# A feed-forward stage of a streaming encoder layer: 18 of 22 gate and up pairs by Strassen's seven block products

## The chip, the core and the metric

The kernel runs on one core of one Trainium2 chip. The metric is device time in microseconds (us) of one execution; lower is better. PE is TensorE's matmul row in the profile, PEld its weight loads, DVE is VectorE, ACT is ScalarE, POOL is GpSimd, SP is SyncE, which issues most of the transfers.

## The reference, cut to what matters

One layer of a hybrid encoder: a half-weighted SwiGLU feed-forward, a conformer convolution beside a Mamba-2 scan, a second half-weighted feed-forward, a final norm. 640 tokens (512 of a prompt and 8 x 16 samples), width 1024, feed-forward width 2816, everything in fp32. What the change touches is the feed-forward alone:

```python
def swiglu_ffn(x, w_gate, w_up, w_down):
    return (jax.nn.silu(x @ w_gate) * (x @ w_up)) @ w_down

x = x + 0.5 * swiglu_ffn(rms_norm(x, norm_ffn1), ffn1_w_gate, ffn1_w_up, ffn1_w_down)
# ... convolution and scan branches, merged ...
x = x + 0.5 * swiglu_ffn(rms_norm(x, norm_ffn2), ffn2_w_gate, ffn2_w_up, ffn2_w_down)
```

## The kernel before

Activations lie transposed, features on the 128 partitions and the 640 tokens (T) along the free axis, in two halves of 320 (TH). A matmul is in a one-pass fp32 format; to keep accuracy each factor is split into a high and a low part, and a product is three matmuls: high x high, high x low, low x high. The high part of a weight block is a cast on ScalarE (`split_hi`, L402), the low part a subtraction on VectorE (`split_lo`, L746).

A **job** (L1192) makes one block of 128 output features for all tokens: 8 chunks of the inner dimension x 3 products x 2 token halves = 48 matmuls of 320 columns, into two PSUM banks of `psj`. Jobs alternate between two buffers b = 0, 1; two jobs with the same number are a **half** (the counter `half` of all semaphores counts pairs of jobs). A feed-forward stage `ffn(f)` has 22 **pairs** (b = 0 gate, b = 1 up) in parts of 8, 8 and 6; behind each part come the 8 down jobs that use its hidden blocks, with 8, 8 or 6 chunks each. The first pair (stage 1: `pair_of_jobs`, L1207, both jobs chunk by chunk) runs on x scaled with the norm's gain but without the norm's root: each gate and up block is multiplied with `rstd` when it leaves PSUM.

Each engine works its own queue in the order written; semaphores connect them. For a pair i VectorE has: the low part of the up weights, `gate_s` = PSUM x rstd (L791), the low part of the next gate weights, `up_s` (L795), `hid` = silu_g x up_s (L799), `h_lo` (L801). ScalarE has: high part, `silu_g` (L434), high part, `h_hi` (L437). A down job ends in `x` += 0.5 x PSUM on VectorE (L820). PE starts a job when its weights' low part is there (`lo_done`) and its buffer has been emptied (`evac_done[b]`):

```python
pe.wait_ge(lo_done, 2 * half + b + 3)
pe.wait_ge(evac_done[b], half + 1)
```

In the first pair the sum of squares is finished (L759), summed over partitions on PE (`token_sums`, L1227), and `rstd` made by VectorE (variance, L763), ScalarE (Ln and Exp, L416 and L418, each behind a load of its table) and three VectorE steps (L769, L771, L773). `gate_s` of the first pair is behind it in VectorE's queue. Weights come by SP in transfers of 512 KB (384 KB for the last down jobs) into `w_raw[b]`, each as soon as the low part of the last one in that buffer is made.

The middle stage between the two feed-forwards (L1285 to L1373 and more jobs of L1202) is not touched, but for the places of its tensors in memory.

## Time and profile before

| | before |
|---|---|
| median of 3 runs | 1932.58 us (1930.64 to 1932.74) |
| the profiled execution | 1932.49 us, its span 1930.7 us |
| PE busy | 1851.6 us (96%), 12359 matmuls |
| PE weight loads | 1807.6 us (94%) |
| DVE busy | 1131.2 us (59%) |
| ACT busy | 735.4 us (38%) |
| granted TensorE clock, mean | 0.972 of 2.4 GHz |
| HBM | 155 MB read, 16 MB written, 89 GB/s |

The span runs from the first to the last instruction of the profiled execution. In the profile's second part a digit is the busy share of a fortieth of the span (48 us) in tenths; stage 1 of the feed-forward is from 9 to 488 us, stage 2 from 1440 to 1918 us.

### The profile page before, as it was taken

To read this page: it belongs to the slowest core of one execution; us is meant where nothing else is said; L and a number is where in the kernel's file an instruction comes from. 1 tells how busy PE (TensorE), PEld (TensorE's weight loads), DVE (VectorE), ACT (ScalarE), POOL (GpSimd) and SP (SyncE) were. 2 spreads that over 40 slices of the span, in tenths; PEclk is the share of its full clock that TensorE was granted. 3 is DMA by queue.
4 is the path that set the end of the run, shared out by engine and by line. 5 is a ranking of instruction groups with operands and counts; after the bars stand their busy time and mean duration, and the time that the engine had idled before them with its cause. 6 is when DMAs were issued, how large, how long until landed. Compare 5 with 4: busy or idle time off the path is not lost.

```text
span 1930.7 us, 29246 instructions
## 1 busy us (share of the span) xinstructions
PE 1851.6 (96%) x12359; PEld 1807.6 (94%) x12359; DVE 1131.2 (59%) x1632; ACT 735.4 (38%) x1306; POOL 94.8 (5%) x149
## 2 busy tenths in 40 slices
PE   6999999999799999989999999998999999999996
PEld 6999999999788999989889998998999999999995
DVE  5342343334647888979898898764544333442344
ACT  5221221122467537635853763254233211221222
POOL 0000000000011011010101101000000000000000
PEclk9999999999899899899989989999999999999998
DMA  4222222223143244134425413231221222222212
GB/s 149 77 77 77 72 76 79 69 74 115 69 125 105 61 153 131 44 118 131 129 53 161 127 49 123 77 127 55 77 77 66 77 77 69 74 77 77 77 63 80
DMA packets 54611, 173.60 MB, mean 90 GB/s; under 512 B 7344, under 2 KB 7504, under 8 KB 54480
## 3 DMA queue, kind: packets, MB, share of 16 engines
q1 hardware_dynamic: 43920, 137.41, 21.0%
q0 software_dynamic: 10560, 34.31, 6.3%
q8 instruction: 98, 1.61, 0.3%
q14 instruction: 33, 0.27, 0.0%
HBM read 155.49 MB, written 16.20 MB: 89 GB/s over the span
## 4 chain that ended last, share of the span: by engine, by line
PE 90%; DVE 4%; ACT 4%; issue 2%; DMA 1%; ACTq 0%; DVEq 0%; SPq 0%; POOLq 0%
PE psj L1202 79%; PE psj L1218 2%; PE pd L1362 2%; PE pc L1343 1%; PE pab L1356 1%; DVE w_lo L746 1%; PE pd L1350 1%; PE pab L1227 1%; ACT w_hi L402 1%; PE pc L1373 1%; PE pd L1373 1%; DVE rstd L773 0%; DVE rstd L771 0%; DVE rstd L769 0%; PE pab L1328 0%
## 5 line engine op out<-in xcount | busy, mean ns | idle before, releaser
L1202 PE MATMUL psj<-xa_hi,w_hi 128*128 128x320 f32 x2592 | 612.1, 318 | 19.4 <-DVE w_lo L746 19.3
L1202 PE MATMUL psj<-xa_lo,w_hi 128*128 128x320 f32 x2592 | 596.6, 312 | 0.0
L1202 PE MATMUL psj<-xa_hi,w_lo 128*128 128x320 f32 x2592 | 595.7, 311 | 0.0
L1202 PEld LDWEIGHTS psj<-xa_hi,w_hi 128*128 128x128 f32 x2592 | 439.7, 190 | 35.2 <-DVE w_lo L746 21.8
L1202 PEld LDWEIGHTS psj<-xa_lo,w_hi 128*128 128x128 f32 x2592 | 439.3, 190 | 0.0
L1202 PEld LDWEIGHTS psj<-xa_hi,w_lo 128*128 128x128 f32 x2592 | 438.5, 190 | 0.0
L746 DVE TENSOR_TENSOR w_lo<-w_raw,w_hi 128x1024 fp32r<-128x1024 f32 (+2 forms) x256 | 292.0, 1140 | 145.0 <-ACT w_hi L402 138.0
L402 ACT CAST w_hi<-w_raw 128x1024 fp32r<-128x1024 f32 (+2 forms) x256 | 250.2, 977 | 283.3 <-PE psj L1202 278.7
L1202 PE MATMUL psj<-h_lo,w_hi 128*128 128x320 f32 x704 | 160.5, 309 | 0.0
L1202 PE MATMUL psj<-h_hi,w_lo 128*128 128x320 f32 x704 | 160.5, 309 | 0.0
L1202 PE MATMUL psj<-h_hi,w_hi 128*128 128x320 f32 x704 | 160.4, 309 | 0.0
L820 DVE SCALAR_TENSOR_TENSOR x<-psj,x 128x640 f32<-128x640 f32 x48 | 39.6, 825 | 170.1 <-PE psj L1202 170.1
L437 ACT CAST h_hi<-hid 128x640 fp32r<-128x640 f32 x44 | 32.1, 730 | 267.6 <-DVE hid L799 267.6
L1202 PEld LDWEIGHTS psj<-h_hi,w_lo 128*128 128x128 f32 x704 | 117.9, 188 | 0.0
L1202 PEld LDWEIGHTS psj<-h_hi,w_hi 128*128 128x128 f32 x704 | 117.9, 188 | 0.0
L1202 PEld LDWEIGHTS psj<-h_lo,w_hi 128*128 128x128 f32 x704 | 117.9, 188 | 0.0
L795 DVE TENSOR_TENSOR up_s<-psj,rstd 128x640 f32<-128x640 f32 x44 | 36.3, 825 | 137.3 <-PE psj L1202 137.3
L924 DVE SCALAR_TENSOR_TENSOR v<-ext_a,parc,v 128x512 f32<-128x512 f32 x240 | 114.7, 548 | 0.0
L924 DVE SCALAR_TENSOR_TENSOR v<-ext_a,parg,v 128x512 f32<-128x512 f32 x240 | 114.4, 548 | 0.0
L434 ACT ACTIVATE silu_g<-gate_s 128x640 f32<-128x640 f32 x44 | 32.6, 740 | 206.6 <-DVE gate_s L791 206.6
L791 DVE TENSOR_TENSOR gate_s<-psj,rstd 128x640 f32<-128x640 f32 x44 | 36.3, 826 | 113.4 <-PE psj L1202 113.3
L948 DVE SCALAR_TENSOR_TENSOR pair<-ext_b,parg,pair 128x512 f32<-128x512 f32 x72 | 53.9, 748 | 37.3 <-ACT ext_b L541 37.0
(218 smaller groups left out, 1968.9 us busy)
## 6 DMA issues: line engine op xcount, KB each, us to landing
w_raw<-in_w_gu SPq DMA_DIRECT2D x88, 512.0 KB, 3.2
w_raw<-in_w_mix SPq DMA_DIRECT2D x56, 512.0 KB, 3.2
w_raw<-in_w_down SPq DMA_DIRECT2D x32, 512.0 KB, 3.2
w_raw<-in_w_tail SPq DMA_DIRECT2D x32, 512.0 KB, 3.2
acb<-cum_dram POOLq DMA_DIRECT2D x20, 512.0 KB, 6.9
w_raw<-in_w_ssm SPq DMA_DIRECT2D x32, 256.0 KB, 2.7
w_raw<-in_w_down_last SPq DMA_DIRECT2D x16, 384.0 KB, 3.0
ach<-cum_dram POOLq DMA_DIRECT2D x40, 128.0 KB, 5.4
```

The lines of the kernel that those rows point to most:

```text
L402: nc.scalar.copy(w_hi[:, b, 0:width], w_raw[:, b, 0:width]).then_inc(hi_done, 1)
L434: nc.scalar.activation(silu_g[:], gate_s[:], ACT.Silu).then_inc(silu_ready, 1)
L746: nc.vector.tensor_tensor(w_lo[:, b, 0:width], w_raw[:, b, 0:width], w_hi[:, b, 0:width].bitcast(F32), ALU.subtract).then_inc(lo_done, 1)
L791: nc.vector.tensor_tensor(halved(gate_s[:]), job_out(0), halved(rstd[:]), ALU.mult).then_inc(evac_done[0], 1)
L795: nc.vector.tensor_tensor(halved(up_s[:]), job_out(1), halved(rstd[:]), ALU.mult).then_inc(evac_done[1], 1)
L820: nc.vector.scalar_tensor_tensor(xc, job_out(b), 0.5, xc, ALU.mult, ALU.add).then_inc(evac_done[b], 1)
L924: nc.vector.scalar_tensor_tensor(dst, src, w[:, w0 + j:w0 + j + 1], dst, ALU.mult, ALU.add).then_inc(conva_ready[c] if s and j == KA - 2 e ...
L948: nc.vector.scalar_tensor_tensor(conv_b[:, s, 0:TP], ext_b[:, s, j:j + TP], param(w0 + j), conv_b[:, s, 0:TP], ALU.mult, ALU.add).then_inc ...
L1202: last = nc.tensor.matmul(psj[:, b, u, 0:TH], w[:, b, cols], act_in[:, k, u * TH:(u + 1) * TH], start=(k == 0 and n == 0), stop=(k == chun ...
L1218: last = nc.tensor.matmul(psj[:, b, u, 0:TH], w[:, b, cols], act_in[:, k, u * TH:(u + 1) * TH], start=(k == 0 and n == 0), stop=(k == chun ...
L1362: last = nc.tensor.matmul(out, old_h[b][:, c * P:(c + 1) * P], bc[:, 1, TP + b * TS:TP + (b + 1) * TS], start=True, stop=True)
L1373: nc.tensor.matmul((pc, pd)[b % 2][:], b_one[b], xtl[:], start=True, stop=True).then_inc(hs_mm, 1)
```

## The change

In each stage the first ORD = 4 pairs stay as they are. The other 18 (runs of 4, 8 and 6, NSP = 18 a stage) are made by Strassen's algorithm in Winograd's form: the weights of a pair are a 2 x 2 matrix of blocks (gate, up; first and second half of the inner dimension), the normed input one of 2 x 2 (halves of the inner dimension; halves of the tokens). Seven products of 4 chunks x 3 matmuls take the place of eight. The products A11, S3, S1 and S2 each begin a bank; A22, A12 and S4 add onto banks that ScalarE has copied out or VectorE has combined in the meantime.

For that the kernel needs: the sums of weight blocks (`sum_sp`, 2048 elements a partition) and the split of 3584 elements a pair in five groups (`split_sp` and `low_sp`, 2048 elements before); combinations of the results on VectorE (`sp_v`, `sp_22`, `sp_21`, `sp_12`), a copy on ScalarE, and the silu in two halves; once a stage the normed input (`normed`, now with rstd), its block sums (`block_sum`) and the split of its seven blocks (`t_high`, `t_low`, 1280 elements each). The weights of a pair come in one transfer of 1 MB (`load_run`), alternately into `w_raw` and a new buffer. The pairs alternate between PSUM banks 0 to 3 (those of `psj`) and 4 to 7. The first pair of each stage leaves PSUM by two copies on ScalarE, and rstd is multiplied in later; half 1's gate weights have a buffer of their own. The load of the dt weights is issued by POOL behind the last product of stage 1. The diff, cut:

```diff
+ORD = 4
+KH = KM // 2
+RUNS = (PARTS[0] - ORD, *PARTS[1:])
+NSP = sum(RUNS)
+FFN_HALVES = ORD + len(PARTS) * (KM // 2)
...
+(Q_A11, Q_S3, Q_S1, Q_S2, Q_A22, Q_A12, Q_S4) = range(7)
+BANK = {Q_A11: 0, Q_S3: 1, Q_S1: 3, Q_S2: 2, Q_A22: 1, Q_A12: 0, Q_S4: 3}
+(X_11, X_T3, X_T1, X_T2, X_T4, X_21, X_22) = range(7)
+X_OF = {Q_A11: X_11, Q_S3: X_T3, Q_S1: X_T1, Q_S2: X_T2, Q_A22: X_T4, Q_A12: X_21, Q_S4: X_22}
+(W_A11, W_S31, W_S2, W_A, W_S4) = range(5)
+W_OF = {Q_A11: W_A11, Q_S3: W_S31, Q_S1: W_S31, Q_S2: W_S2, Q_A22: W_A, Q_A12: W_A, Q_S4: W_S4}
...
+            def load_run(f, r, first):
+                for j in range(RUNS[r]):
+                    n = NSP * f + sum(RUNS[0:r]) + j
+                    before = sp_before(n, sp_buffer)
+                    if before is not None:
+                        sp.wait_ge(sp_lo, 5 * before + 4)
+                    if j == 1:
+                        sp.wait_ge(lo_done, 2 * first + 2)
+                    if f == 1 and n == NSP:
+                        sp.wait_ge(job_done, 2 * FFN2_HALF + 4)
+                    sp.dma_start(sp_raw(n)[:] if sp_buffer(n) else sp_raw(n),
+                                 d["w_sp"][n]).then_inc(sp_raw_in[sp_buffer(n)], 16)
...
+            def split_sp(n, w):
...
+                if w in (W_A11, W_A):
+                    b = sp_buffer(n)
+                    act.wait_ge(sp_raw_in[b], 16 * len([m for m in range(n + 1) if sp_buffer(m) == b]))
+                else:
+                    act.wait_ge(sp_sum, 3 * n + {W_S31: 1, W_S2: 2, W_S4: 3}[w])
+                if n:
+                    act.wait_ge(sp_done, 7 * (n - 1) + {W_A11: 1, W_S31: 3, W_S2: 4, W_A: 6, W_S4: 7}[w])
...
+                nc.scalar.copy(group_of(w_hi_4, w3_hi, w), fp32_of(n, w)).then_inc(sp_hi, 1)
...
+                act.wait_ge(job_done, 2 * half + 3)
+                act.wait_ge(acc_ready, (Q_FFN1, Q_FFN2)[f] + KM)
+                nc.scalar.copy(halved(gate_s), job_out(0)).then_inc(evac_done[0], 1)
+                act.wait_ge(job_done, 2 * half + 4)
+                nc.scalar.copy(halved(up_s), job_out(1)).then_inc(evac_done[1], 1)
+                split_hi(half + 1, 1)
+                inverse_root((N_FFN1, N_FFN2)[f], 7 * f)
+                silu(0)
+                split_hi(half + 2, 0)
+                silu(1)
+                split_hi(half + 2, 1)
+                t_high(X_11, 4)
+                silu(2)
+                split_hi(half + 3, 0)
+                t_high(X_T3, 9)
+                t_high(X_T1, 10)
+                split_hi(half + 3, 1)
+                t_high(X_T2, 11)
+                t_high(X_T4, 12)
+                t_high(X_21, 8)
+                t_high(X_22, 8)
+                n0 = NSP * f
+                split_sp(n0, W_A11)
+                for i in range(ORD - 1):
+                    h_high(i, hid_buf[:, i], i)
+                silu(3)
+                split_sp(n0, W_S31)
+                split_sp(n0, W_S2)
+                split_sp(n0, W_A)
+                split_sp(n0, W_S4)
+                h_high(3, hid, 3)
...
+                    for j in range(length):
+                        n = n0 + j
+                        more = j + 1 < length
+                        if j:
+                            split_sp(n, W_S4)
+                            act.wait_ge(sp_c12, n)
+                            nc.scalar.activation(silu_g[:, TH:T], c12, ACT.Silu).then_inc(sp_silu, 1)
+                        if more:
+                            split_sp(n + 1, W_A11)
+                        if j:
+                            h_high(i0 + j - 1, hid, chunk0 + j - 1)
+                        act.wait_ge(sp_done, 7 * n + 2)
+                        if n:
+                            act.wait_ge(sp_d, n)
+                        if not j:
+                            act.wait_ge(hid_ready, q0 + i0)
+                        nc.scalar.copy(halved(mix_c), ps[:, sp_set(n):sp_set(n) + 2, 0:TH]).then_inc(sp_copied, 1)
+                        if more:
+                            split_sp(n + 1, W_S31)
+                            split_sp(n + 1, W_S2)
+                            split_sp(n + 1, W_A)
+                        else:
+                            split_hi(half, 0, PARTS[r] * P)
+                            split_hi(half, 1, PARTS[r] * P)
+                        act.wait_ge(sp_done, 7 * n + 6)
+                        act.wait_ge(hid_ready, q0 + i0 + j)
+                        nc.scalar.activation(silu_g[:, 0:TH], ps[:, sp_set(n), 0:TH], ACT.Silu).then_inc(sp_silu, 1)
...
+            def sum_sp(n, w):
+                raw, b = sp_raw(n), sp_buffer(n)
+                if n % NSP == 0:
+                    dve.wait_ge(hlo_ready, NFF * (n // NSP) + ORD - 1)
+                if n:
+                    dve.wait_ge(sp_lo, 5 * (n - 1) + w + 1)
+                    dve.wait_ge(sp_sum, 3 * (n - 1) + {W_S31: 2, W_S2: 3, W_S4: 3}[w])
+                if w == W_S31:
+                    dve.wait_ge(sp_raw_in[b], 16 * len([m for m in range(n + 1) if sp_buffer(m) == b]))
+                    nc.vector.tensor_tensor(w_sum[:, 0:2], raw[:, 1:3], raw[:, 0].unsqueeze(1).broadcast_to([P, 2, KH * P]),
+                                            ALU.add).then_inc(sp_sum, 1)
+                elif w == W_S2:
+                    dve.wait_ge(sp_sum, 3 * n + 1)
+                    nc.vector.tensor_tensor(w_sum[:, 2], w_sum[:, 1], raw[:, 1], ALU.add).then_inc(sp_sum, 1)
+                else:
+                    dve.wait_ge(sp_sum, 3 * n + 2)
+                    nc.vector.tensor_tensor(w_sum[:, 3], w_sum[:, 2], raw[:, 3], ALU.add).then_inc(sp_sum, 1)
+            def low_sp(n, w):
+                dve.wait_ge(sp_hi, 5 * n + w + 1)
+                nc.vector.tensor_tensor(group_of(four_lo, w3_lo, w), fp32_of(n, w),
+                                        group_of(four_hi, w3_hi, w).bitcast(F32), ALU.subtract).then_inc(sp_lo, 1)
...
+            def sp_v(n):
+                dve.wait_ge(sp_copied, n + 1)
+                dve.wait_ge(sp_done, 7 * n + 4)
+                if n:
+                    dve.wait_ge(sp_c12, n)
+                nc.vector.tensor_tensor(halved(mix_d), halved(mix_c), ps[:, sp_set(n) + 2:sp_set(n) + 4, 0:TH],
+                                        ALU.subtract).then_inc(sp_d, 1)
+            def sp_22(n, before):
+                dve.wait_ge(sp_d, n + 1)
+                dve.wait_ge(hhi_ready, before)
+                dve.wait_ge(hlo_ready, before)
+                nc.vector.tensor_tensor(hid[:, TH:T], mix_d[:, TH:T], mix_d[:, 0:TH], ALU.subtract).then_inc(sp_c22, 1)
+            def sp_21(n):
+                dve.wait_ge(sp_done, 7 * n + 5)
+                nc.vector.tensor_tensor(hid[:, 0:TH], bank(n, 1), mix_d[:, 0:TH], ALU.subtract).then_inc(sp_c21, 1)
+            def sp_12(n):
+                dve.wait_ge(sp_done, 7 * n + 7)
+                dve.wait_ge(sp_silu, 2 * n)
+                nc.vector.tensor_tensor(c12, bank(n, 3), mix_d[:, 0:TH], ALU.add).then_inc(sp_c12, 1)
+            def sp_hid(n):
+                dve.wait_ge(sp_c22, n + 1)
+                dve.wait_ge(sp_c21, n + 1)
+                dve.wait_ge(sp_silu, 2 * n + 2)
+                nc.vector.tensor_tensor(hid, silu_g, hid, ALU.mult).then_inc(hid_ready, 1)
...
+                def normed(c):
+                    cols = slice(c % KH * TH, (c % KH + 1) * TH)
+                    out = t_sum[:, X_11:X_T4 + 1:X_T4 - X_11, cols] if c < KH else t_sum[:, X_21:X_22 + 1, cols]
+                    nc.vector.scalar_tensor_tensor(out, halved(x[:, c]), gains[:, 2 * f:2 * f + 1, c],
+                                                   halved(rstd[:]), ALU.mult, ALU.mult).then_inc(t_step, 1)
...
+                variance((N_FFN1, N_FFN2)[f], DM, RMS_EPS)
+                split_lo(half + 1, 1)
+                newton(7 * f)
+                dve.wait_ge(evac_done[0], half + 2)
+                nc.vector.tensor_tensor(gate_s, gate_s, rstd[:], ALU.mult).then_inc(scaled, 1)
+                dve.wait_ge(evac_done[1], half + 2)
+                nc.vector.tensor_tensor(up_s, up_s, rstd[:], ALU.mult).then_inc(scaled, 1)
...
+                hidden(0)
+                gate(1)
+                split_lo(half + 2, 0)
+                normed(0)
+                normed(1)
+                up(1)
+                hidden(1)
+                split_lo(half + 2, 1)
+                for c in range(2, KM):
+                    normed(c)
+                gate(2)
+                split_lo(half + 3, 0)
+                block_sum(X_T3, X_T4, X_22, ALU.subtract, 8)
+                block_sum(X_T1, X_11, X_T4, ALU.subtract, 8)
+                up(2)
+                hidden(2)
+                split_lo(half + 3, 1)
+                block_sum(X_T2, X_22, X_T1, ALU.add, 10)
+                block_sum(X_T4, X_21, X_T2, ALU.subtract, 11)
+                t_low(X_11)
+                n0 = NSP * f
+                low_sp(n0, W_A11)
+                t_low(X_T3)
+                t_low(X_T1)
+                for i in range(ORD - 1):
+                    h_low(i, hid_buf[:, i], i)
+                gate(3)
+                sum_sp(n0, W_S31)
+                sum_sp(n0, W_S2)
+                low_sp(n0, W_S31)
+                t_low(X_T2)
+                low_sp(n0, W_S2)
+                up(3)
+                hidden(3)
+                t_low(X_T4)
+                sum_sp(n0, W_S4)
+                low_sp(n0, W_A)
+                h_low(3, hid, 3)
+                t_low(X_21)
+                low_sp(n0, W_S4)
+                t_low(X_22)
...
+                    for j in range(length):
+                        n = n0 + j
+                        more = j + 1 < length
+                        if j:
+                            sp_12(n - 1)
+                        if more:
+                            sum_sp(n + 1, W_S31)
+                        if j:
+                            sp_hid(n - 1)
+                            low_sp(n, W_S4)
+                        if more:
+                            low_sp(n + 1, W_A11)
+                            sum_sp(n + 1, W_S2)
+                        if j:
+                            h_low(i0 + j - 1, hid, chunk0 + j - 1)
+                        if more:
+                            sum_sp(n + 1, W_S4)
+                            low_sp(n + 1, W_S31)
+                        sp_v(n)
+                        sp_22(n, q0 + i0 + j)
+                        if more:
+                            low_sp(n + 1, W_S2)
+                        else:
+                            split_lo(half, 0, PARTS[r] * P)
+                        sp_21(n)
+                        if more:
+                            low_sp(n + 1, W_A)
+                        else:
+                            split_lo(half, 1, PARTS[r] * P)
...
+                def product(n, q):
+                    pe.wait_ge(sp_lo, 5 * n + W_OF[q] + 1)
+                    if n % NSP == 0:
+                        pe.wait_ge(t_lo_ready, 7 * f + X_OF[q] + 1)
+                    first = q in (Q_A11, Q_S3, Q_S1, Q_S2)
+                    if first:
+                        before = sp_before(n, sp_set)
+                        if before is not None:
+                            pe.wait_ge(sp_c12, before + 1)
+                            pe.wait_ge(sp_silu, 2 * before + 2)
+                    else:
+                        pe.wait_ge(sp_copied if q != Q_S4 else sp_d, n + 1)
+                    hi, lo = block_of(four_hi, w3_hi, q), block_of(four_lo, w3_lo, q)
+                    for k in range(KH):
+                        for m, (w, t) in enumerate(((hi, t_hi), (hi, t_lo), (lo, t_hi))):
+                            last = nc.tensor.matmul(ps[:, sp_set(n) + BANK[q], 0:TH], w[:, k * P:(k + 1) * P],
+                                                    t[:, X_OF[q], k * TH:(k + 1) * TH],
+                                                    start=(first and k == 0 and m == 0),
+                                                    stop=(k == KH - 1 and m == 2), skip_group_check=not first)
+                    last.then_inc(sp_done, 1)
...
+                    for j in range(RUNS[p]):
+                        if j < 2:
+                            pe.wait_ge(evac_done[0], half + 1)
+                            pe.wait_ge(evac_done[1], half + 1)
+                        for q in range(7):
+                            product(n0 + j, q)
```

## Rows read from the trace of the kernel before

**Rows 1.** The page: busy us and share; then 40 slices of PE and its clock.

```profile
PE 1851.6 (96%) x12359; PEld 1807.6 (94%) x12359; DVE 1131.2 (59%) x1632; ACT 735.4 (38%) x1306; POOL 94.8 (5%) x149
...
PE   6999999999799999989999999998999999999996
PEclk9999999999899899899989989999999999999998
```

**Rows 2.** The chain that ended last: start us, us, what; stage 2.

```profile
1457.86 452.38 PE psj L1202 x3072
```

**Rows 3.** Timeline of PE, stage 2: start us, us, instructions.

```profile
1453.42 0.46 PE L1202 MATMUL psj<-xa_hi,w_lo 128*128 128x320 f32 x2
1457.86 0.57 PE L1202 MATMUL psj<-xa_hi,w_hi 128*128 128x320 f32 x2 [3.98 <-DVE w_lo L746]
...
1462.73 0.46 PE L1202 MATMUL psj<-xa_hi,w_lo 128*128 128x320 f32 x2
...
1469.47 0.46 PE L1202 MATMUL psj<-xa_lo,w_hi 128*128 128x320 f32 x2
```

**Rows 4.** Windows: us, PE, PEld, DVE, ACT, POOL busy, PEclk, DMA share, GB/s.

```profile
45.00:143.00 98.00, 98.00 (x670) 98.00 (x670) 39.86 (x42) 23.49 (x28) 0.00 (x0) 1.00 0.22 75
...
590.00:605.00 15.00, 15.00 (x121) 13.92 (x119) 13.41 (x23) 12.66 (x36) 3.88 (x6) 1.00 0.60 175
```

**Rows 5.** Chain and groups of instructions, line 1343, middle stage.

```profile
604.18 1.02 PE pc L1343 x16
...
L1343 PE MATMUL pc<-mdec,xdt 128*64 128x128 f32 x320 | 22.8, 286 | 7.0 <-issue 7.0
```

**Rows 6.** Groups by form: busy us, mean ns of one, idle before; the two splits.

```profile
L746 DVE TENSOR_TENSOR w_lo<-w_raw,w_hi 128x1024 fp32r<-128x1024 f32 x208 | 254.7, 1225 | 141.5 <-ACT w_hi L402 134.5
...
L746 DVE TENSOR_TENSOR w_lo<-w_raw,w_hi 128x512 fp32r<-128x512 f32 x32 | 22.0, 687 | 0.0
...
L402 ACT CAST w_hi<-w_raw 128x1024 fp32r<-128x1024 f32 x208 | 217.3, 1045 | 201.8 <-PE psj L1202 197.4 <-DVE yb L1098 4.3
...
L402 ACT CAST w_hi<-w_raw 128x512 fp32r<-128x512 f32 x32 | 19.7, 616 | 81.5 <-PE psj L1202 81.2 <-DMA w_raw<-in_w_ssm 0.2
```

**Rows 7.** Timeline of DVE and of ACT in the first pair of stage 1.

```profile
15.22 0.88 DVE L778 SCALAR_TENSOR_TENSOR xa_lo<-x,gains,xa_hi 128x640 fp32r<-128x640 f32 x1
16.02 0.82 DVE L759 TENSOR_TENSOR acc<-acc,sq 128x640 f32<-128x640 f32 x1
...
18.28 0.88 DVE L778 SCALAR_TENSOR_TENSOR xa_lo<-x,gains,xa_hi 128x640 fp32r<-128x640 f32 x1
...
16.07 0.81 ACT L421 ACTIVATE xa_hi<-x,gains 128x640 fp32r<-128x640 f32 x1
```

**Rows 8.** Groups by form on ACT: two copies out of PSUM.

```profile
L656 ACT COPY z<-psj 128x640 f32<-128x640 f32 x16 | 11.0, 687 | 4.0 <-PE psj L1202 4.0
...
L536 ACT COPY ext_b<-psj 128x320 f32<-128x320 f32 x24 | 10.0, 415 | 0.0
```

**Rows 9.** Timeline of PE and of DVE at a job's end.

```profile
135.90 0.46 PE L1202 MATMUL psj<-h_hi,w_hi 128*128 128x320 f32 x2
...
136.10 0.82 DVE L795 TENSOR_TENSOR up_s<-psj,rstd 128x640 f32<-128x640 f32 x1 [3.24 <-PE psj L1202]
```

**Rows 10.** Timeline of PE, stage 1: end of the first pair, next job.

```profile
26.88 0.46 PE L1218 MATMUL psj<-xa_hi,w_lo 128*128 128x320 f32 x2
35.72 0.91 PE L1202 MATMUL psj<-xa_hi,w_hi 128*128 128x320 f32 x2 [8.38 <-DVE w_lo L746]
...
39.09 0.47 PE L1202 MATMUL psj<-xa_hi,w_hi 128*128 128x320 f32 x2
```

**Rows 11.** Timeline of ACT and DVE: stage 2's norm, from the exponential's table on.

```profile
1449.37 1.28 ACT L418 ACT_TABLE_LOAD   x1
1450.67 0.74 ACT L418 ACTIVATE pair<-pair 128x640 f32<-128x640 f32 x1
...
1452.30 0.82 DVE L771 TENSOR_TENSOR rstd<-rstd,pair 128x640 f32<-128x640 f32 x1
```

441 lines of the change are left out of this document (283 added, 158 removed).

## The prediction

> **What bounds the kernel now.** I read the page first. TensorE's matmul row is busy 96% of the span while VectorE has 59% and ScalarE 38%, and nearly every slice outside the two ends and the middle stands at 9 with the granted clock at 9 tenths or more [rows 1]. A busy PE row alone doesn't prove that PE sets the time, so the chain of waits comes next: each feed-forward stage is in it one unbroken piece of 3072 matmuls, 452.38 us long for stage 2 and 0.02 less for stage 1 [rows 2]. Inside it a pair of 128x320 matmuls starts every 0.293 us: 23 such pairs between 1462.73 and 1469.47 give 6.74/46 = 0.1465 us (0.1466 with the decimals of more rows) for one matmul at the full 2.4 GHz [rows 3], and 3072 x 0.1466 = 450.4 is all of the piece but 2.0. So in these stages nothing but the number of matmuls sets the time, no wait is left but one at each stage's start, and a window of the first stage has PE busy 98.00 of 98 us, VectorE 39.86, ScalarE 23.49 [rows 4]. These are what the change can spend.
>
> **Matmuls removed.** A pair now is two jobs of 8 chunks x 3 products x 2 token halves = 96 matmuls, 14.07 us. A changed pair has 7 products of 4 chunks x 3 = 84, 12.31 us. 36 pairs lose 12 each: 432 x 0.1466 = **-63.3 us**. What the two shapes differ in beside that is where a matmul writes: before, neighbours alternate between two banks, now 12 in a row add into the same one. No row shows that. The nearest is the 16 matmuls of line 1343, which go to one bank in 1.02 us, 0.064 each, though each record lasts 0.286 [rows 5]; a bank does not hold the next matmul until the last is written. They write other columns of it and do not add, so the ends are 0 and, if each waited for the end of a record of that length, 3024 x 0.14 = +420 us. I take 0: the nearest row shows no hold at all. The products' extra semaphore waits cost nothing where they are met: the jobs on the hidden blocks wait at each of their chunks of 6 matmuls and lie inside the same unbroken piece [rows 2].
>
> **What a run of changed pairs asks of VectorE.** From the two forms of the split, 1024 elements take 1.225 us and 512 take 0.687 [rows 6]: 0.15 + 1.05 ns an element, which fits the 0.82 shown for 640 [rows 7]; so 320 is taken as 0.49 and 1280 as 1.50. Where nothing is awaited, the next operation starts 0.09 before the recorded end of the last (0.88 at 15.22, the next at 16.02 [rows 7]). A pair needs 3 of 1024 (sum S3/S1, two splits), 5 of 512, 3 of 640 (difference, product, low part of the hidden block) and 3 of 320: 3.68 + 3.44 + 2.48 + 1.47 = 11.1 us by durations, 14 x 0.09 less = 9.8 by pitch, in 12.31 us of PE. ScalarE: 2 x 1.045 + 3 x 0.616 for the splits, 0.69 for the copy, 0.72 for the hidden block (the casts give 0.838 ns an element), 2 x about 0.42 for the half silus, as a copy of 320 [rows 6, 8] = 6.2 us. Both fit. The order matters as much: call t = 0 the start of a pair n on PE. ScalarE's last split for pair n+1 waits for the product A12 (10.56), ends 11.6, and VectorE, which stands in its queue at the low part of it, gets on at 11.65 and ends at 12.8, i.e. 0.5 into the next pair. From there to the end of the difference that product S4 needs lie 1 of 320, 2 of 1024, 3 of 640 and 4 of 512 by pitch, 7.3, with a wait of some 0.5 for the high part of S3/S1 at 6.35: done at 8.4, and PE wants it at 10.56. **2.1 us of slack**; by full durations 1.8 us is left. So I cost the runs at 0, with VectorE as the engine that would be late next. The weights come in one transfer of 1 MB a pair, issued about 12 us ahead: 85 GB/s beside 75 now at a DMA share of 0.22 [rows 4]. The transfer of the dt weights that POOL now issues behind the last product of stage 1 has the last 8 down jobs, 8 x 36 x 0.1466 = 42 us, as cover. The split put early into stage 1's prologue delays ScalarE's next inputs by 1.0 us, where it is 2.2 us ahead of VectorE (input 6: 16.07 against 18.28 [rows 7]): nothing.
>
> **After a down stage.** The first changed pair of a run writes the banks of the last down job, so it waits for the update of x. Now jobs alternate and nothing waits. From PE's last matmul to VectorE's start are 0.20 us (135.90 to 136.10), the update lasts as long as this operation, 0.82 [rows 9], and about 0.1 passes to PE: 1.13, four times: **+4.5 us**.
>
> **The start of each stage, taken away.** Now PE stands after the first pair, because its banks are emptied only with rstd: from 27.17 (26.88 + 2 matmuls) to 35.72, 8.55 us, and from 1453.71 to 1457.86, 4.15 us [rows 3, 10]. After each gap PE runs some matmuls at 1.2 GHz (0.267 a matmul): 12 in 3.37 us where 1.76 are due, and 22 in 4.87 where 3.23 are due, so 1.6 more each [rows 3, 10]. In the new kernel ScalarE copies the banks out without rstd. In stage 2 the first bank is free during the second job: the gap goes. In stage 1 both jobs end together: 0.2 + 0.69 + 0.06 = 0.95 stays, and I expect no half clock after it. **-(7.6 + 4.15 + 3.2) = -15.0 us**.
>
> **The start of each stage, added.** Before the first changed pair VectorE must scale the input, form the block sums of x and split all 7 of them, in the time of 3 ordinary pairs. Let T be the end of the first pair; then PE has work to T + 42.2 in stage 2, T + 43.2 in stage 1. rstd is later than now: ScalarE first copies (0.2 to 0.9) and splits (1.9), then loads a table (1.28), Ln (0.74), a table, Exp: 6.0 [rows 11]; three VectorE steps of 0.82 that read one another, 0.86 with the gap: **T + 8.6** (9.25 in stage 1). From there to up(3), the emptying of the last bank that the first product waits for, VectorE's queue holds 14 operations of 640 (2 scalings, 3 gates, 3 ups, 3 hidden, 3 low parts) x 0.74 = 10.4; 8 input scalings of 0.80 = 6.4; 6 of 1024 x 1.14 = 6.8; 8 of 1280 (4 block sums, 4 low parts) x 1.41 = 11.3; 3 of 512 x 0.60 = 1.8: 36.7. It stands for ScalarE four times: 1.9 for the high part of (3,0), 0.9 for that of (3,1), 3.15 at the first A11 split, which stands behind four casts of 1.26 on ScalarE, and 0.5 for S3/S1; and 0.12 more in each of some 6 steps that read the one before. 36.7 + 6.45 + 0.7 = 43.8, so up(3) ends at **T + 52.4**, though its job is done at 42.2. up(3) stands behind sums, splits and low parts that the first product does not need, and behind the wait of VectorE all of PE is queued. PE's stall: 10.15 in stage 2, 53.05 - 43.2 = 9.85 in stage 1. After it the clock has fallen as after the 8.38 gap [rows 10]: 1.6 each. Then VectorE has 13.5 us to the difference of pair 0 (the four things left over, 7 splits and sums of pair 1), T + 65.9, where PE wants to begin S4 at 52.4 + 10.56 + 1.6 = 64.6: 1.3 each. Together **20.0 + 3.2 + 2.6 = +25.8 us**. Bounds: by recorded durations instead of pitches 38 x 0.09 = 3.4 more in each stage and some 2 more at S4 (+11 in all); if the waits for ScalarE are half as long and the clock holds, 3 + 1.6 less each (-9).
>
> As to the pitch, the Trainium skill (VectorE: DVE Perf Modes, "The DRAIN you can't avoid") says that a next operation starts only once the pipe has emptied, whether or not a semaphore stands between. The trace has the next start 0.09 ahead of the recorded end even with a met wait between [rows 7]; by a reading of that rule that puts operations end to end the time would be the +11 above.
>
> **Sum** against the profiled execution (1932.49, its span 1930.7; the median of the runs is 1932.58, the same): -63.3 - 15.0 + 4.5 + 25.8 = -48.0, **1884 us**. Stage 1 comes out some 26 us shorter, stage 2 some 22, the rest as it is.
>
> **The rivals.**
> A, the forecast: PE-bound runs, one stall of about 10 us at each stage's start. 0.63.
> B, the starts cost little (VectorE faster through its queue, PE held only a few us): without the 25.8 it would be 1859; with a third of it 1867. For it: VectorE was idle over half of this stretch before. Against it: the queue is in order and up(3) is its 39th entry. 0.10.
> C, VectorE end to end at recorded durations: 1884 + 11 = 1895, and up to 1905 if single pairs lose a few tenths. For it: nearly every new operation carries a wait. Against it: the start at 16.02 [rows 7]. 0.15.
> D, slower: VectorE is late in each pair, and PE's gap before S4 drops the clock. Needed is that the way from the low part of A to the difference, 7.8 by pitch with its wait, grows beyond 9.9 (a quarter more). If then each of the 36 pairs pays 1.6 at 1.2 GHz and a few tenths of waiting, say 1.9, it is 1884 + 68 = 1952; it decides from 48.0/36 = 1.33 us a pair. For it: after 8.4 and after 4.0 us of waiting the clock did fall [rows 3, 10]. Against it: in the middle stage PE changes between groups of 24 and fewer matmuls with a wait at each, VectorE 89% busy, and the granted clock is 1.00 [rows 4]. 0.07. The Trainium skill (TensorE: Matmul & The Clock Gate, "A second HAM failure mode: psum-queue depth-cycling") tells of a kernel whose short idle times between matmul groups made the clock swing; by it the 252 products with their waits would bring this case. That window does not agree with it for groups of this size.
> E, adding into one bank 12 times in a row slows the matmul: 16 ns each (11%) on 3024 eats all 48.0 us. Also slower then, 1935 or above. 0.05.
> That the change does not do what it says I leave out: the loops give 84 matmuls.
>
> **How the numbers follow.** The likeliest is A, 1884. A's own bounds are 1875 to 1895; C adds 1905, B 1859. 1867 to 1902 leaves out D, E, half of B and the end of C, about 0.2. About 0.2% (4 us) is what a measurement can tell from no change. Faster: A, B, C and a share of E: 0.90. Same: 0.02. Slower: D and most of E, 0.08.
>
> **What would show it.** PE has 11927 matmuls. Within the runs a product takes 12 x 0.1466 = 1.76 us and 7 of them 12.3 with no gap. PE stands about 1 us after stage 1's first pair and not at all in stage 2. One gap of about 10 us before the first product of each stage, released by VectorE's up_s, 1.2 GHz for some 12 matmuls behind it. A gap of about 1.1 us at the start of the other four runs, released by the update of x. VectorE about 80 to 90% busy in the runs. Wrong would be: gaps before S4 in each pair, a pitch above 0.147 in the products, a clock under 1.00 in the runs, or a start gap far from 10.

## The result and the profile after

The changed kernel takes **1884.68 us** (median of 4 runs, 1880.54 to 1889.88) beside 1931.61 (1929.54 to 1932.74) for the kernel before on the same chip: ratio 0.976, 95% interval 0.9733 to 0.9786. The profiled execution took 1883.59 us, its span is 1881.8. The prediction was 1884.

The page: busy us, share, instructions; then the slices of PE, DVE and the clock, as in [rows 1].

```profile
PE 1789.4 (95%) x11927; PEld 1742.4 (93%) x11927; DVE 1331.1 (71%) x1958; ACT 853.0 (45%) x1504; POOL 94.8 (5%) x149
...
PE   7799999998899999999999999998999799999996
...
DVE  6863873774648888989899899765556854863754
...
PEclk9899999999889899899999989999999899999998
```

432 matmuls fewer, as counted. The cost shows in PE's slices: a 7 in the second slice and in the thirty-second where before there were 9s, each with an 8 in the clock row. VectorE is up from 59% to 71%.

The chain of waits (start us, us, what) has the stages in pieces now, where [rows 2] was a single one:

```profile
26.98 37.33 PE ps L1564 x252
...
132.54 56.32 PE ps L1564 x384
188.86 0.96 issue
189.82 98.79 PE ps L1625 x672
...
1472.73 6.40 issue
1479.13 52.32 PE ps L1625 x336
...
1587.77 0.96 issue
1588.73 98.79 PE ps L1625 x672
```

L1625 is the products' matmul, L1564 that of plain and down jobs. 98.79 us for 672 matmuls, eight pairs of 84, is 0.1470 us each, and 12.35 us a pair. The down jobs have 56.32/384 = 0.1467.

Windows over the run of eight in stage 1, and over the time before the first product (columns as in [rows 4]):

```profile
190.00:288.00 98.00, 98.00 (x669) 98.00 (x669) 75.55 (x104) 46.05 (x69) 0.00 (x0) 1.00 0.22 79
...
72.00:82.00 10.00, 1.79 (x7) 1.82 (x8) 9.55 (x11) 3.25 (x4) 0.00 (x0) 0.50 0.00 0
```

In the run PE is busy throughout at a granted clock of 1.00 and VectorE 77%. In the other PE stands until 80.21 and VectorE is busy 9.55 of 10 us: the whole start waits for it.

PE's timeline at both stage starts, and what PE waited for in all (us in total, times, longest):

```profile
80.21 0.61 PE L1625 MATMUL ps<-t_hi,w_hi 128*128 128x320 f32 x1 [10.64 <-issue]
...
93.58 0.39 PE L1625 MATMUL ps<-t_hi,w_hi 128*128 128x320 f32 x1 [0.17 <-DVE sq L1010]
...
1479.13 0.61 PE L1625 MATMUL ps<-t_hi,w_hi 128*128 128x320 f32 x1 [10.64 <-issue]
1479.53 0.47 PE L1625 MATMUL ps<-t_lo,w_hi 128*128 128x320 f32 x1
...
1484.60 0.47 PE L1625 MATMUL ps<-t_hi,w_lo 128*128 128x320 f32 x1
1484.87 0.38 PE L1625 MATMUL ps<-t_hi,w_hi 128*128 128x320 f32 x1
1485.09 0.31 PE L1625 MATMUL ps<-t_lo,w_hi 128*128 128x320 f32 x1
```
```profile
PE ps L1625 <- issue: 25.1, 6, 10.6
```

The profile names nobody ("issue") for the long wait. VectorE's timeline does: up(3) (L1047) ends 0.2 us before PE's start. From 1479.53 on a matmul comes every 0.267 us, until 1484.87; the granted clock from 1479.13 to there is 0.50 of 2.4 GHz, which is 1.2 GHz. The six waits of the products in this line are 2 x 10.64 + 4 x 0.96, and only 0.2 us of their waiting is outside it.

```profile
79.19 0.81 DVE L1047 TENSOR_TENSOR sq<-ps,rstd 128x640 f32<-128x640 f32 x1
```

**Where the time went**, by the traces. The end of a group of matmuls is taken as the start of its last one and 0.147 us. From the end of the first pair to the end of the last down job stage 1 took 460.7 us (27.17 to 487.91) and takes 435.3 (26.81 to 462.12): -25.4. Stage 2 took 456.4 (1453.71 to 1910.06) and takes 435.3 (1425.70 to 1861.04): -21.0. What lies between them is 2.2 shorter, the time up to the end of the first pair 0.4, the tail 0.1 longer: -48.9 in all, as the spans have it (1930.7 and 1881.8). The end of stage 1's first pair in the changed kernel, and the job behind it:

```profile
26.52 0.46 PE L1582 MATMUL ps<-xa_hi,w_lo 128*128 128x320 f32 x2
26.97 0.53 PE L1564 MATMUL ps<-xa_hi,w_hi 128*128 128x320 f32 x2
```

### The profile page after: what moved, and what is told of

It is laid out like the page before. It is cut to its first block, busy times and chain, and to the rows that moved or that the text cites. A ratio compares the mean times of both kernels' runs of the same rounds, so it can differ in the third digit from the quotient of the medians.

```text
span 1881.8 us, 29519 instructions
## 1 busy us (share of the span) xinstructions
PE 1789.4 (95%) x11927; PEld 1742.4 (93%) x11927; DVE 1331.1 (71%) x1958; ACT 853.0 (45%) x1504; POOL 94.8 (5%) x149
## 3 DMA queue, kind: packets, MB, share of 16 engines
q8 instruction: 95, 1.56, 0.3%
## 4 chain that ended last, share of the span: by engine, by line
PE 84%; DVE 7%; ACT 5%; issue 3%; DMA 1%; DVEq 0%; ACTq 0%; SPq 0%; POOLq 0%
PE ps L1564 52%; PE ps L1625 23%; PE ps L1582 3%; PE ps L1760 2%; PE ps L1771 1%; DVE v L1287 1%; DVE w_lo L942 1%; PE ps L1754 1%; PE ps L1741 1%; PE ps L1748 1%; PE ps L1591 1%; ACT w_hi L510 1%; DVE t_lo L1078 1%; ACT acb L778 1%; DVE pair L1311 0%
## 5 line engine op out<-in xcount | busy, mean ns | idle before, releaser
L1564 PE MATMUL ps<-xa_hi,w_hi 128*128 128x320 f32 x1440 | 348.5, 324 | 7.1 <-DVE w_lo L942 7.0
L1625 PE MATMUL ps<-t_hi,w_hi 128*128 128x320 f32 x1008 | 314.5, 312 | 25.3 <-issue 25.1
L1564 PE MATMUL ps<-xa_lo,w_hi 128*128 128x320 f32 x1440 | 332.7, 313 | 0.0
L1564 PE MATMUL ps<-xa_hi,w_lo 128*128 128x320 f32 x1440 | 332.4, 312 | 0.0
L1625 PE MATMUL ps<-t_lo,w_hi 128*128 128x320 f32 x1008 | 313.6, 311 | 0.0
L1625 PE MATMUL ps<-t_hi,w_lo 128*128 128x320 f32 x1008 | 313.6, 311 | 0.0
L1564 PEld LDWEIGHTS ps<-xa_hi,w_hi 128*128 128x128 f32 x1440 | 246.2, 192 | 23.2 <-issue 12.7
L1564 PEld LDWEIGHTS ps<-xa_lo,w_hi 128*128 128x128 f32 x1440 | 245.3, 191 | 0.0
L1564 PEld LDWEIGHTS ps<-xa_hi,w_lo 128*128 128x128 f32 x1440 | 245.0, 191 | 0.0
L1625 PEld LDWEIGHTS ps<-t_hi,w_hi 128*128 128x128 f32 x1008 | 191.3, 190 | 27.1 <-issue 27.1
L1625 PEld LDWEIGHTS ps<-t_lo,w_hi 128*128 128x128 f32 x1008 | 191.3, 190 | 0.0
L1625 PEld LDWEIGHTS ps<-t_hi,w_lo 128*128 128x128 f32 x1008 | 191.2, 190 | 0.0
L1564 PE MATMUL ps<-h_lo,w_hi 128*128 128x320 f32 x704 | 160.5, 309 | 0.0
L1564 PE MATMUL ps<-h_hi,w_hi 128*128 128x320 f32 x704 | 160.4, 309 | 0.0
L1564 PE MATMUL ps<-h_hi,w_lo 128*128 128x320 f32 x704 | 160.3, 309 | 0.0
L1564 PEld LDWEIGHTS ps<-h_hi,w_lo 128*128 128x128 f32 x704 | 117.7, 188 | 0.0
L1564 PEld LDWEIGHTS ps<-h_lo,w_hi 128*128 128x128 f32 x704 | 117.7, 188 | 0.0
L1564 PEld LDWEIGHTS ps<-h_hi,w_hi 128*128 128x128 f32 x704 | 117.6, 188 | 0.0
```

Of the source, the lines that this page charges most:

```text
L1564: last = nc.tensor.matmul(psj[:, b, u, 0:TH], w[:, cols], act_in[:, k, u * TH:(u + 1) * TH], start=(k == 0 and n == 0), stop=(k == chunks ...
L1625: last = nc.tensor.matmul(ps[:, sp_set(n) + BANK[q], 0:TH], w[:, k * P:(k + 1) * P], t[:, X_OF[q], k * TH:(k + 1) * TH], start=(first and ...
```

## The experiments

The theory is the prediction's: PE-bound runs, in which VectorE has some 2 us of slack a pair, and at each stage's start one stall because VectorE is late. Open after the result are: what makes VectorE late (the place of up(3) in its queue, or the queue's length); whether the slack is what I said; whether a late VectorE would have dropped the clock (rival D); and what the copies of the first pair give by themselves.

| kernel | median, us | ratio to before, 95% interval |
|---|---|---|
| the change | 1884.68 | 0.9733 to 0.9786 |
| e1, up(3) early | 1884.35 | 0.9742 to 0.9785 |
| e2, six plain pairs | 1864.96 | 0.9640 to 0.9682 |
| e3, 1.56 us more VectorE work a pair | 1885.44 | 0.9721 to 0.9784 |
| e4, 3.12 us more | 1899.54 | 0.9812 to 0.9868 |
| e5, five plain pairs | 1861.57 | 0.9617 to 0.9652 |
| e6, before with the copies alone | 1919.54 | 0.9918 to 0.9950 |
| e7, 4.16 us more | 1923.99 | 0.9964 to 0.9993 |
| e8, 6.24 us more | 2003.76 | 1.0353 to 1.0410 |
| e9, e5 with one wait less | 1863.27 | 0.9645 to 0.9684 |
| e10, e9 with one low part later | 1859.54 | 0.9610 to 0.9649 |

### e1: up(3) moved forward

```diff
                 low_sp(n0, W_A11)
+                gate(3)
                 t_low(X_T3)
+                up(3)
                 t_low(X_T1)
                 for i in range(ORD - 1):
                     h_low(i, hid_buf[:, i], i)
-                gate(3)
                 sum_sp(n0, W_S31)
                 sum_sp(n0, W_S2)
                 low_sp(n0, W_S31)
                 t_low(X_T2)
                 low_sp(n0, W_S2)
-                up(3)
                 hidden(3)
```

> Only VectorE's order at each stage's start is changed: gate(3) and up(3) stand right behind the split of A11 and one low part, so the last bank is free about 1 us after its job. Theory Q (the stall is the whole length of VectorE's queue up to the difference of pair 0; in the changed kernel that difference ends at T + 67.4, with PE only 0.3 us in front of it): the gap before the first product shrinks from 10.6 to about 1 us, but new gaps stand before S3, A22 and the others, and S4 of pair 0 begins only 1 to 2 us earlier; 1881 to 1884 us. Theory P (the stall is the place of up(3) in the queue, as the prediction names it, and all of it goes with the place): 2 x (10.6 + 2.5) less, about 1858 us.

Measured: 1884.35 us, no change. PE's timeline in stage 1, all waits of the first changed pair, and the end of VectorE's difference:

```profile
71.48 0.38 PE L1625 MATMUL ps<-t_hi,w_hi 128*128 128x320 f32 x1 [1.58 <-DVE t_lo L1078]
78.48 0.64 PE L1625 MATMUL ps<-t_hi,w_hi 128*128 128x320 f32 x1 [5.02 <-DVE w_lo L998]
93.90 0.60 PE L1625 MATMUL ps<-t_hi,w_hi 128*128 128x320 f32 x1 [4.12 <-DVE sq L1010]
```
```profile
92.94 0.81 DVE L1010 TENSOR_TENSOR sq<-sq,ps 128x640 f32<-128x640 f32 x1
```

The stall of 10.64 became three of 1.58, 5.02 and 4.12, sum 10.72, and product S4 starts at 93.90 where it started at 93.58. PE began 8.7 us earlier and gained nothing: the difference stands at the end of the same queue. So what sets the end of the start phase is the length of VectorE's queue up to the difference. The place of up(3) only says where PE does its waiting.

### e2: six plain pairs in place of four

```diff
-ORD = 4
+ORD = 6
```

with the queues of ScalarE and VectorE spread over the two further pairs, and two more buffers for hidden blocks. Each stage does 24 matmuls more, and PE has 28 us more of plain work in which VectorE can catch up.

> Six ordinary pairs at each stage's start in place of four, 16 Strassen pairs in place of 18, the same work of VectorE for the input spread over two more pairs. Theory Q (VectorE's backlog): it has 28 us more of PE's time as cover and adds only 2 x 5.3 us of its own, so the gap of 10.6 us, the half clock of 2.5 and the 0.3 before S4 go, and 4 pairs cost 1.76 us more each: -26.7 + 7.0 = -19.7, about 1865 us, no gap over 1.5 us before the first product. Rival (the gap belongs to the hand-over from jobs to products and not to VectorE's backlog): it stays, 1884.7 + 7.0 = 1892 us.

Measured: 1864.96, 20 us under the change.

```profile
26.10 70.75 PE ps L1585 x480
96.86 2.04 issue
98.90 25.09 PE ps L1646 x168
```

In stage 1 the products start after 2.04 us of waiting in place of 10.64, and 168 matmuls in 25.09 us are 0.149 each: no half clock. In stage 2 they start after 2.06 us, and there the clock did fall:

```profile
1487.12 0.52 PE L1646 MATMUL ps<-t_hi,w_hi 128*128 128x320 f32 x1 [2.06 <-issue]
...
1490.64 0.31 PE L1646 MATMUL ps<-t_lo,w_hi 128*128 128x320 f32 x1
```

13 matmuls take 3.5 us where 1.9 are due, 1.6 lost. Stage 1 has -8.6 of waiting, -2.5 of half clock, -0.3 before S4 and +3.5 of matmuls, -7.9; stage 2 has -8.6, -1.1 and +3.5, -6.2; -14.1 for both, and from the end of the first pair to the last down job the traces differ by -7.7 and -6.3. The spans differ by 17.8 (1881.8 and 1864.0). The other 3.9 lie outside the two stages, 0.9 before the end of the first pair and 3.0 in the middle stage, whose work the edit leaves as it is; their cause is open.

### e3 and e4: more work for VectorE in each pair

Both leave the computation whole and add operations whose result nobody reads; of the 36 changed pairs 30 get them, behind `h_low` (e3: three, e4: six):

```diff
+                            for _ in range(3):
+                                if filled[0]:
+                                    dve.wait_ge(filler, filled[0])
+                                nc.vector.tensor_tensor(acc[:, TH:T], rstd[:, 0:TH], rstd[:, TH:T],
+                                                        ALU.add).then_inc(filler, 1)
+                                filled[0] += 1
```

> Three operations of 320 elements more on VectorE in each Strassen pair but the first of a run (30 pairs), each waiting for the one before: 0.52 us each, 1.56 a pair. They compute nothing that is used. Theory (2 us of slack between the difference and S4): no change, 1884.7 within its noise, PE without gaps in the runs, the difference ends at about 9.8 us into the pair. Rival (VectorE's queue already bounds the pair): 30 x 1.56 = +47 us, 1931.

> Six such operations a pair, 3.1 us, more than the slack. Theory: the difference ends about 1.0 us after PE wants S4, so each of the 30 pairs is some 1.0 us longer and nothing else happens: 1884.7 + 30 = 1915 us, granted clock 1.00 in the runs. Rival D of the prediction (the short gap before S4 in each pair drops TensorE's clock): 1.6 to 2.5 us more in each pair, 1963 to 1990 us, clock well under 1.00 in the runs.

Measured: e3 1885.44, no change; e4 1899.54, +15. PE's waits on the difference in e3 and then in e4:

```profile
PE ps L1632 <- DVE sq L1011: 1.3, 1, 1.3
```
```profile
PE ps L1632 <- DVE sq L1011: 13.1, 26, 1.3
```

The one wait of e3 stands before S4 of stage 2's first pair (1499.01), which has no added operation; the pairs that have them show none. Of e4's 26 two are such waits at the stage starts (1.3 us each), the other 24 last 0.4 to 0.5 us. So 1.56 us fit and 3.12 don't; the slack is between, where the prediction had it at 2.1. But e4 should have cost 1.0 a pair and cost 0.63. Its VectorE timeline shows why, from one difference to the next:

```profile
214.02 0.81 DVE L1011 TENSOR_TENSOR sq<-sq,ps 128x640 f32<-128x640 f32 x1
214.86 0.49 DVE L1018 TENSOR_TENSOR pair<-sq 128x320 f32<-128x320 f32 x1
215.27 0.69 DVE L999 TENSOR_TENSOR w_lo<-w_sum,w_hi 128x512 fp32r<-128x512 f32 x1
215.87 0.48 DVE L1022 TENSOR_TENSOR pair<-ps,sq 128x320 f32<-128x320 f32 x1
216.27 1.22 DVE L999 TENSOR_TENSOR w_lo<-raw_b,w_hi 128x1024 fp32r<-128x1024 f32 x1
...
222.22 3.13 DVE L1156 TENSOR_TENSOR acc<-rstd 128x320 f32<-128x320 f32 x6
...
227.00 0.81 DVE L1011 TENSOR_TENSOR sq<-sq,ps 128x640 f32<-128x640 f32 x1
```

In the change VectorE waits 1.8 us ahead of this low part of A and 0.41 or more ahead of the one for S3/S1:

```profile
214.10 1.23 DVE L998 TENSOR_TENSOR w_lo<-raw_b,w_hi 128x1024 fp32r<-128x1024 f32 x1 [1.79 <-ACT w_hi L548]
```

In e4 there is no wait left: the period is 12.98 (214.02 to 227.00), from start to start 3.04 of added operations (222.22 to 225.26) and 9.94 of the pair's own work. The expectations of e7 and e8, written with 9.83 and 0.52 for each added operation, come to the same within 0.06. My sum had kept the low part of A tied to the end of product A12 and forgotten that once PE waits, that wait of VectorE vanishes too. **A pair lasts as long as the longer of PE's 12.35 us and VectorE's whole queue**, and the slack is 12.35 - 9.94 = 2.4 us. The window says that the clock held, against rival D (e4, a wait of 0.4 to 0.5 us in each pair):

```profile
190.00:288.00 98.00, 94.42 (x635) 92.78 (x634) 91.64 (x142) 46.31 (x67) 0.00 (x0) 1.00 0.22 76
```

### e7 and e8: longer waits in each pair

The same edit with eight and twelve operations.

> As e4_fill6, with eight added VectorE operations of 0.52 us in each of 30 of the 36 changed pairs (4.16 us). The formula that e4 left: a pair lasts as long as the longer of TensorE's 12.35 and VectorE's queue, 9.83 + the added work: 13.99 us here, +1.04 a pair on e4's 1899.5: 1931, with an idle time of TensorE of about 1.7 us in each pair. If the clock falls after idle times of that length, as the forecast's rival D had it, the granted clock in a window of the runs is under 1.00, and the time is up to 1.6 us a pair more, 1979.

> As e7_fill8 with twelve operations (6.24 us): a pair of 9.83 + 6.24 = 16.07 us, 3.12 a pair more than e4, 1993, with TensorE idle about 3.7 us in each pair. The idle time of 4.15 us in the kernel before was followed by 22 matmuls at 1.2 GHz, so here the granted clock of the runs should be under 1.00. Theory (VectorE's queue is the period): the slower matmuls are absorbed in TensorE's slack and the time stays at 1993. Rival (the loss adds to the period, because the last split waits for TensorE's product A12): 1993 + 30 x 1.6 = 2041.

Measured: e7 1923.99, e8 2003.76. The windows of e7, then of e8:

```profile
190.00:288.00 98.00, 88.08 (x592) 86.44 (x591) 91.24 (x143) 42.99 (x62) 0.00 (x0) 1.00 0.19 65
```
```profile
190.00:288.00 98.00, 85.00 (x537) 83.83 (x536) 84.06 (x134) 35.42 (x52) 0.00 (x0) 0.93 0.20 71
```

e7: differences start at 216.03 and 230.06, a period of 14.03 (forecast 13.99), PE waits 1.5 to 1.6 us in each of 24 pairs, and the clock stays at 1.00. The time is 7 under the forecast, which counted 30 pairs. The last pair of each run has no next pair to prepare, so its queue is short and it shows no wait; 24 remain: 24 x (13.99 - 12.35) = 39 on 1884.7 is 1924, as measured. The same count makes e4 24 x 0.63 = 15, as measured. I made this count after the result of e7, so that the two times fit it is less than a forecast; the periods of 12.98 and 14.03 don't depend on it.

e8 does drop the clock. After the 3.69 us at 226.58 the slow matmuls begin at once; after the 2.78 us at 244.27 the first seven keep the full speed and 13 matmuls at 1.2 GHz follow from 245.37:

```profile
226.58 0.60 PE L1632 MATMUL ps<-t_hi,w_hi 128*128 128x320 f32 x1 [3.69 <-DVE sq L1011]
226.98 0.47 PE L1632 MATMUL ps<-t_lo,w_hi 128*128 128x320 f32 x1
...
244.27 0.39 PE L1632 MATMUL ps<-t_hi,w_hi 128*128 128x320 f32 x1 [2.78 <-DVE sq L1011]
```

Neither is a rule. The 24 long waits of e8 are ten of 2.8 us and 14 of 3.2 to 3.7; matmuls at 1.2 GHz follow on all of the 14 (twice only after five to nine at full speed) and on five of the ten.

The expectation's two times were 1993 (the slow matmuls absorbed) and 2041 (paid), and the measured 2003.76 is nearer to the first. With 24 pairs in place of 30 they are 1884.7 + 24 x 3.72 = 1974 and 1974 + 24 x 1.6 = 2012, and it is nearer to the second. The trace decides. PE's waits on the difference in e8:

```profile
PE ps L1632 <- DVE sq L1011: 79.5, 31, 3.7
```

Of the 119 us over the change 79.5 are waits. The slow matmuls behind 19 of the 24 long waits, summed one by one, take 33 us more than at full speed. They are mostly paid: where the clock fell VectorE waits for PE in turn (1.06 us ahead of 230.15) and the period is 17.69 or 16.87 us, where it did not fall (277.06 to 293.19) it is 16.13, the queue's own length, and 24 x (16.13 - 12.35) would be 91 us in all, 28 under what e8 costs. So rival D's second half was sound: with waits of about 3 us in every pair the clock falls behind most of them, and that is paid for. Its first half was not: waits of 0.4 to 1.6 us do nothing to the clock.

### e6: the kernel before with the copies alone

ScalarE copies the first pair out and `rstd` is multiplied in later; the splits of the second pair's weights stand ahead of the norm's root. Everything else is the kernel before.

```diff
+                            job_ended(half + i, 0)
+                            nc.scalar.copy(halved(gate_s[:]), job_out(0)).then_inc(evac_done[0], 1)
...
+                            job_ended(half + i, 1)
+                            nc.scalar.copy(halved(up_s[:]), job_out(1)).then_inc(evac_done[1], 1)
...
+                            nc.vector.tensor_tensor(gate_s[:], gate_s[:], rstd[:], ALU.mult).then_inc(scaled, 1)
```

> The kernel before, eight products for every pair, with one thing of the change alone: at the start of each feed-forward stage ScalarE copies the first pair out of the accumulators, and the factor of the norm is multiplied in later. If the wait at the start of a stage was that of PSUM banks held until the factor is there: the idle time in stage 1 falls from 8.55 to about 4 (the next weights are split behind the copies; the stretch at half clock stays), in stage 2 from 4.15 to 0 with its half-clock stretch of 1.6: together -10.3, about 1921. Rival (the wait is only moved: the factor's chain comes later and the next pair's banks are held for it): within 3 us of 1931.

Measured: 1919.54, ratio 0.9934: about 13 us by the medians (10 to 16 by the interval, 9.7 between the two profiled spans), a quarter of what the whole change brings, has nothing to do with the products.

```profile
28.86 0.65 PE L1228 MATMUL psj<-xa_hi,w_hi 128*128 128x320 f32 x2 [2.99 <-DVE w_lo L761]
...
1463.64 0.56 PE L1228 MATMUL psj<-xa_hi,w_hi 128*128 128x320 f32 x2 [2.22 <-DVE w_lo L761]
```

Beside [rows 10] and [rows 3]: 8.38 fell to 2.99 in stage 1. In stage 2 the gap of 3.98 went from behind the first pair, as forecast, but one of 2.22 us came behind the second: VectorE takes its gate out of PSUM only at 1459.80, behind four operations on the first pair, and the low part that PE waits for comes after. The half clock behind the gap of stage 2 is gone.

### e5, e9 and e10: five plain pairs

> Five pairs by eight products start each feed-forward stage (runs of 3, 8 and 6 pairs in seven), with the first product of the first run in banks 4 to 7, so that it waits for no plain pair's product, and the queues of ScalarE and VectorE reordered for that. Against e2_ord6 (1864.96) this trades one plain pair for one of seven products in each stage: 24 matmuls fewer in all, of 0.1466 us, -3.5. My working: idle time at the start of the first run near 0 (e2: 2.04), at its third product about 0.6, at its fourth about 0.7, so 1.3 of idle time a stage where e2 has 2.04. Sum about -3.5 - 1.5 = -5: about 1860, no stretch at the lower clock there. Rival (the backlog of VectorE comes back, since one more product of the plain pairs is still being worked off when the run starts): waits of 3 to 4 us in the first pair of the run and the same time or worse than e2, 1865 to 1870.

> e5_ord5 with one wait of TensorE mended. The text on e5_ord5 said that its first product writes banks 4 to 7 and waits for no plain pair; the banks were so, but the wait for both emptied banks still stood before it, and the trace of e5 has the product start 0.21 us after up(4) ends (84.68 to 84.89), 1.71 us after TensorE was free. Here only the products that write banks 0 to 3 wait for it. Theory (VectorE's queue sets it, with no idle time in it from 70.8 on): the stall moves. Product A11 starts at once, S3 waits 0.8 us for the low part of S3/S1 (VectorE ends it at 85.7, wanted at 84.9) and S4 waits 0.9 for the difference, which ends at 95.5 as before: same time as e5, within 1 us. Rival (the wait for up(4) was what held TensorE): 1.7 us less in each stage, -3.4, about 1858.

> e9_ord5_banks, and in the first pair of each stage's first run VectorE makes the low part of the next pair's S3/S1 (1.14 us) behind the difference in place of before it. If VectorE's queue sets the start of S4, the difference ends at 94.4 in place of 95.5 in stage 1, S4 starts at 94.6, when TensorE is there: 1.07 us less in each stage, -2.1 on e5 (about 1859.5), with the 0.8 us at S3 left. If it does not, the same as e9.

e5 is `ORD = 5` with queues of its own. e9 changes one line of it, e10 one more place:

```diff
-                        if j < 2:
+                        if j < 2 and not sp_set(n0 + j):
```
```diff
-                            low_sp(n + 1, W_S31)
+                            if r or j:
+                                low_sp(n + 1, W_S31)
                         sp_v(n)
+                        if not r and not j:
+                            low_sp(n + 1, W_S31)
```

Measured: 1861.57, 1863.27 and 1859.54. The waits at the start of stage 1 in e5, in e9 and in e10:

```profile
84.89 0.39 PE L1633 MATMUL ps<-t_hi,w_hi 128*128 128x320 f32 x1 [1.71 <-issue]
```
```profile
85.84 0.42 PE L1633 MATMUL ps<-t_hi,w_hi 128*128 128x320 f32 x1 [0.95 <-DVE w_lo L1001]
95.65 0.39 PE L1633 MATMUL ps<-t_hi,w_hi 128*128 128x320 f32 x1 [0.73 <-DVE sq L1013]
```
```profile
85.37 0.42 PE L1636 MATMUL ps<-t_hi,w_hi 128*128 128x320 f32 x1 [0.95 <-DVE w_lo L1001]
```

e5 kept a wait for up(4) that its banks do not need (its expectation says otherwise and is wrong there). Taking it away in e9 turns 1.71 into 0.95 + 0.73 = 1.68: e1 again, in small. Only when the queue ahead of the difference is made shorter by one operation, in e10, does 0.73 go. Whole-run times can't tell the three apart, their intervals overlap; the traces do. The lowest median is that of e10, 1859.54 us, ratio 0.9629 to the 1928.63 of the kernel before beside it: 69 us under that, and 25 under the changed kernel.

## Why the prediction was right

**The sum and its terms.** -48.0 predicted, -48.9 measured. Term by term:

| step | predicted | measured |
|---|---|---|
| a product's matmul | 0.1466 us | 0.1470 |
| stage 1 / stage 2 | -26 / -22 | -25.4 / -21.0 |
| wait after the first pair, stage 1 / 2 | 0.95 / 0 | 0.16 / 0 |
| up(3) ends, stage 1 / 2 | T + 53.05 / 52.4 | T + 53.2 / 53.2 |
| the stall before the first product | 9.85 / 10.15 | 10.64 / 10.64 |
| half clock behind it, each | 1.6 | 2.5 / 2.7 |
| wait before S4 of the first pair | 1.3 | 0.3 / 0 |
| wait after a down stage, x 4 | 1.13 | 0.96 |
| the rest of the kernel | 0 | -2.5 |

T is the end of the first pair (26.81 in stage 1, 1425.70 in stage 2). The half clock of stage 2 is read from the row of 1479.13: 21 matmuls to 1484.87 take 5.74 where 21 x 0.1466 = 3.08 are due.

**Adding into one bank** 12 times in a row costs nothing that shows: 0.1470 against 0.1467 in the down jobs. Rival E is refuted.

**VectorE in the runs.** The difference ends 8.64 us into the pair by the rows of the pair that begins at 202.14 (predicted 8.4), and VectorE's work from start to start is 9.94 in e4 (predicted 9.8). The rows behind the first number:

```profile
208.82 1.22 DVE L998 TENSOR_TENSOR w_lo<-w_sum,w_hi 128x1024 fp32r<-128x1024 f32 x1 [0.41 <-ACT w_hi L548]
209.97 0.81 DVE L1010 TENSOR_TENSOR sq<-sq,ps 128x640 f32<-128x640 f32 x1
210.81 0.49 DVE L1017 TENSOR_TENSOR pair<-sq 128x320 f32<-128x320 f32 x1
```

The difference (209.97) begins 0.07 before the recorded end of the low part ahead of it (208.82 + 1.22 = 210.04). The next one, which reads the difference, begins 0.03 behind its recorded end (209.97 + 0.81). So an operation waits for the end of the one before where it reads its result, and not else; the difference in start is 0.10 us. That speaks against rival C: its +11 us did not come. The Trainium skill (VectorE: DVE Perf Modes, "The DRAIN you can't avoid") says that the next operation waits until the pipe is empty, and adds what the prediction left out, that one which is not held starts earlier. The 0.07 above agree with the addition and not with the reading that puts all operations end to end.

**The clock in the runs.** 1.00 in every window of the change. The Trainium skill's oscillation (TensorE: Matmul & The Clock Gate, "A second HAM failure mode: psum-queue depth-cycling") does not show here, nor at waits of 0.5 us (e4) or 1.6 us (e7) in every pair. In e8, with waits of 2.8 to 3.7 us in every pair, the clock does go to and fro (0.93).

**What was wrong.** First, the cause of the stall as the prediction put it: it named up(3)'s place behind work that the first product does not need. The number was right since it came from the queue's length; the reason would have led to the edit of e1, which brings nothing.

Second, sizes at the stage starts. The wait after stage 1's first pair was taken as 0.95, for both jobs ending together. But the last chunk's gate matmuls end 0.88 before its up matmuls, so ScalarE's copy of the gate was done by 26.83 and the next job began at 26.97, 0.16 after the pair. The stall of stage 1 is larger by the same 0.8: up(3) ends at T + 53.2, about as forecast, but PE ran out of work at T + 42.6, not 43.2. VectorE's waits for ScalarE on the way to up(3) were taken as 6.45; in stage 2 those four are 5.6, and a fifth, 1.5 before the first hidden block, had been left out.

The half clock was taken as 1.6 after the gap of 8.38 [rows 10], and was 2.5 and 2.7; the wait at S4 was taken as 1.3, and was 0.3 and 0. These two are linked, and how they divide changes from run to run: behind the same stall of 10.64 the traces of e3, e4, e7 and e8, which have the same stage start, show 10 to 21 slow matmuls, a loss of 1.3 to 2.6 us, and where the loss is 1.3 to 1.5 the wait at S4 is 1.2 to 1.3. In all ten starts of these five traces S4 begins 13.4 us after the first product, since VectorE's queue sets it; so only their sum counts, 2.9 forecast and 2.7 measured.

Third, the prediction left the rest of the kernel as it is, and 2.5 us went there: 2.2 in the middle stage and 0.4 before the end of the first pair, whose 84 matmuls take 14.47 us in place of 15.27 but begin 0.45 later; the tail gave 0.1 back. This covers what the stages brought less than forecast (1.6), which is luck. Runs of one kernel differ by up to 9 us (1880.54 to 1889.88), so I make nothing of it; no run took it apart.

Fourth, the rule by which rival D priced a late VectorE (the low part of A stays tied to PE) is refuted by e4: the price is the excess of the whole queue over PE's time, and slow matmuls come on top only when the waits are long (e8).

**Not tried:** a first pair of products with fewer splits of x (the block sums' low parts are 7 of the 38 entries), and a lighter rstd chain.
